# Expert weights in paired rows, a later combine, a spill from ScalarE's queue, and idle-time matmuls in a mixture-of-experts block

## The reference, cut to what matters

```python
h = rmsnorm(x, g_pre_ffn) * (1 + sc2) + sh2
logits = h @ w_router + b_router            # 256 x 32
top_v, top_i = lax.top_k(logits, 4)
gates = softmax(top_v)
# for each expert e, for the tokens that chose it:
gu = xblk @ w_gate_up[e] + b_gate_up[e]     # 1024 x 2048
x_glu = minimum(gu[:, :1024], 7.0)
x_lin = clip(gu[:, 1024:], -7.0, 7.0)
act = x_glu * sigmoid(1.702 * x_glu) * (x_lin + 1)
y = act @ w_down[e] + b_down[e]             # 1024 x 1024
out[token] += y * gate
x = x + gt2 * rmsnorm(out, g_post_ffn)
```

## Time and profile before

| | |
|---|---|
| median of 3 runs | 1250.05 us |
| profiled execution: its own time | 1251.14 us |
| its span, first to last instruction | 1249.1 us |
| PE (TensorE matmul) busy | 1037.8 us, 83% |
| PEld (weight load) busy | 496.9 us, 40% |
| DVE / ACT / POOL busy | 291.9 / 184.7 / 30.4 us |
| DMA moved | 464.63 MB, mean 372 GB/s |
| main DMA queue, share of 16 engines' span | 91.8% |
| chain that ended last | PE 52%, DMA 38%, DVE 4%, issue 3%, ACT 1% |
| mean granted TensorE clock | 0.935 |

### The profile page before, as it was taken

The page is one execution under the profiler, slowest core; times in us unless marked ns, Lnnn a source line. Parts: engine busy times, 40 slices in busy tenths (PEclk is TensorE's granted clock), DMA queues, the critical chain, the costliest instruction groups (busy, mean ns, idle before and its releaser), DMA issues.

```text
span 1249.1 us, 21341 instructions
## 1 busy us (share of the span) xinstructions
PE 1037.8 (83%) x8279; PEld 496.9 (40%) x8280; DVE 291.9 (23%) x786; ACT 184.7 (15%) x459; POOL 30.4 (2%) x52
## 2 busy tenths in 40 slices
PE   2799999977775999789979996999799979696965
PEld 0565878643332334324333433343334333232322
DVE  6646522142121111211121112112111211111112
ACT  0311354031011101011101110111011101100112
POOL 1000100130000000000000000000000000000000
PEclk9799999978888999989998999999899989898988
DMA  9979721977999969999999999999999999999996
GB/s 353 381 268 400 294 101 47 412 289 294 415 418 418 417 235 419 418 417 390 419 419 417 376 420 418 418 384 419 418 418 382 418 418 418 417 418 418 417 418 243
DMA packets 92208, 464.63 MB, mean 372 GB/s; under 512 B 5166, under 2 KB 6998, under 8 KB 59292
## 3 DMA queue, kind: packets, MB, share of 16 engines
q1 hardware_dynamic: 91740, 462.76, 91.8%
q0 software_dynamic: 448, 1.59, 0.3%
HBM read 462.22 MB, written 2.11 MB: 372 GB/s over the span
## 4 chain that ended last, share of the span: by engine, by line
PE 52%; DMA 38%; DVE 4%; issue 3%; ACT 1%; POOL 0%; DVEq 0%; SPq 0%; ACTq 0%; POOLq 0%
DMA arena<-in_w_down_dram 35%; PE pp L1402 15%; PE pp L1374 13%; PE pp L1182 4%; PE pp L1104 4%; DMA arena<-in_w_ada_dram 3%; PE po L1330 3%; PE pp L1195 2%; PE po L1247 2%; PE pp L1343 2%; PE pp L1363 2%; DVE arena L747 1%; PE pp L1382 1%; PE po L1062 1%; PE pp L1350 1%
## 5 line engine op out<-in xcount | busy, mean ns | idle before, releaser
L1374 PE MATMUL pp<-arena,work 128*32 128x256 f32 (+1 forms) x3840 | 360.1, 430 | 8.6 <-DMA arena<-in_w_gate_up_dram 8.6
L1402 PE MATMUL pp<-arena,work 128*32 128x256 f32 (+1 forms) x1920 | 217.7, 487 | 121.1 <-DMA arena<-in_w_down_dram 90.7
L1374 PEld LDWEIGHTS pp<-arena,work 128*32 128x32 f32 (+1 forms) x3840 | 155.8, 116 | 210.3 <-issue 140.7
L1402 PEld LDWEIGHTS pp<-arena,work 128*32 128x32 f32 (+1 forms) x1920 | 79.3, 128 | 220.3 <-DMA arena<-in_w_down_dram 111.1
L967 DVE TENSOR_SCALAR work<-pp 128x128 f32<-128x128 f32 (+1 forms) x74 | 25.3, 342 | 445.7 <-PE pp L1374 445.7
L669 ACT ACTIVATE work<-work 128x128 f32<-128x128 f32 (+1 forms) x74 | 25.9, 350 | 398.1 <-DVE work L967 398.1
L1343 PE MATMUL pp<-h_sb,work 128*32 128x256 f32 (+1 forms) x480 | 54.6, 462 | 34.1 <-issue 29.8
L1330 PE MATMUL po<-work 64*128 64x512 f32 x304 | 79.0, 640 | 1.6 <-ACT work L683 1.6
L961 DVE COPY work<-pp 128x256 f32<-128x256 f32 (+1 forms) x37 | 19.5, 526 | 234.7 <-PE pp L1343 234.7
L1182 PE MATMUL pp<-arena 128*128 128x256 f32 x256 | 57.4, 382 | 0.0
L747 DVE SCALAR_TENSOR_TENSOR arena<-arena,small 128x1024 f32<-128x1024 f32 x42 | 54.0, 1285 | 9.2 <-DMA arena<-in_w_ada_dram 7.7
(11 more groups left out here) (207 smaller groups left out, 643.7 us busy)
## 6 DMA issues: line engine op xcount, KB each, us to landing
arena<-in_w_gate_up_dram SPq DMA_DIRECT2D x128, 2048.0 KB, 25.6
arena<-in_w_down_dram SPq DMA_DIRECT2D x64, 2048.0 KB, 25.1
arena<-in_w_ada_dram SPq DMA_DIRECT2D x12, 2048.0 KB, 12.8
arena<-in_w_in_dram SPq DMA_DIRECT2D x5, 2048.0 KB, 15.7
arena<-in_w_gate_dram SPq DMA_DIRECT2D x4, 2048.0 KB, 14.2
arena<-in_w_out_dram SPq DMA_DIRECT2D x2, 2048.0 KB, 10.0
arena<-in_w_branch_a_dram SPq DMA_DIRECT2D x1, 2048.0 KB, 18.4
arena<-in_w_branch_b_dram SPq DMA_DIRECT2D x1, 2048.0 KB, 17.3
```

Of the source, the lines that this page charges most:

```text
L1374: mm = t_.matmul(pp[j * m:(j + 1) * m, UP[hh], 0:w].rearrange("p (s f) -> p s f", s=2), hgT[:, at:at + m], gu_w[slot][:, k, :, col:col + w ...
L1402: mm = t_.matmul(pp[j * m:(j + 1) * m, UP[0], 0:w], actT[:, at:at + m], wd[:, j * w:(j + 1) * w], start=(n == 0), stop=(n == KD - 1))
```

## The change

Six edits, made together:

- **Paired rows.** The contraction rows of an expert's matrices are dealt to partitions in pairs: partition p takes rows 256g + 2p and 256g + 2p + 1. A load of gate/up is then 128 runs of 16 KB in place of 256 of 8 KB, and a load of `w_down` 256 runs of 8 KB in place of 512 of 4 KB. The gathered tokens and the activations are turned in steps of two to match, and a narrow block's gate/up halves are the even and the odd columns: its moving operand is read with a step of two elements.
- **Order in a block.** `combine` and the turning of the scatter matrix move behind gate/up; the bias products move ahead of the turning of the tokens. `turn_half(1)` runs ahead of the down product. `actT` gets its own place. The bias is loaded twice, to two groups of rows (`hh`), so that the bias products of the halves stand in different rows.
- **Spill.** `x1` is written to DRAM from ScalarE's queue, after its squares, in place of SyncE's.
- **Tables.** `grids` moves from `bgu` into `gain2`; `gain2` (one row) is first written to DRAM by GpSimd and read back at the end (512 KB, behind `x1_back`). GpSimd makes the tables after its sums of the merged branches. DVE waits for them (`s_places`).
- **DVE order.** `first_part` stands ahead of the second `weigh` of its tile.
- **Products on idle TensorE.** `spin`: 16 products of zeros into `po` bank 0 in the routing chain, and 14 products into a free `pp` bank behind it.

```diff
 PAGE = 4096
+PAIR = 2 * P
...
-def bias_rows_of(slot):
-    return slice(32 + 64 * slot, 32 + 64 * slot + NBR)
+def bias_rows_of(slot, hh):
+    return slice(64 * slot + 32 * hh, 64 * slot + 32 * hh + NBR)
...
         bgu = sb("bgu", [96 + NBR, 2, BR])
-        grids = bgu[0:NEXP, :, :].rearrange("p s f -> p (s f)").rearrange("p (n e) -> p n e", e=NEXP)
+        grids = gain2[0:NEXP, 0:16 * NEXP].rearrange("p (n e) -> p n e", e=NEXP)
...
         hgT = work[:, 384:896]
-        actT = work[:, 384:896]
+        actT = work[:, 2176:2688]
...
-        gu_v = w_gate_up[0].rearrange("e (k p) n -> e p k n", p=P)
-        dn_v = w_down[0].rearrange("e (k p) n -> e p k n", p=P)
+        gu_v = w_gate_up[0].rearrange("e (g p r) n -> e p g (r n)", p=P, r=2)
+        dn_v = w_down[0].rearrange("e (g p r) n -> e p g (r n)", p=P, r=2)
...
             def load_bgu(slot, e):
-                sp.dma_start(bgu[bias_rows_of(slot), :, :], bgu_v[e]).then_inc(s_bgu[slot], 16)
+                for hh in range(2):
+                    sp.dma_start(bgu[bias_rows_of(slot, hh), :, :], bgu_v[e]).then_inc(s_bgu[slot], 16)
 
             def load_gu(slot, e, i):
-                sp.dma_start(gu_w[slot][:, 2 * i:2 * i + 2, :, :].rearrange("p k s f -> p k (s f)"),
-                             gu_v[e, :, 2 * i:2 * i + 2, :]).then_inc(s_gup[slot][i], 16)
+                sp.dma_start(gu_w[slot][:, 2 * i:2 * i + 2, :, :].rearrange("p k s f -> p (k s f)"),
+                             gu_v[e, :, i, :]).then_inc(s_gup[slot][i], 16)
...
             def load_dlo(slot, e):
-                sp.dma_start(dlo_w[slot], dn_v[e, :, 0:4, :]).then_inc(s_dlo[slot], 16)
+                sp.dma_start(dlo_w[slot].rearrange("p (g r) d -> p g (r d)", r=2),
+                             dn_v[e, :, 0:2, :]).then_inc(s_dlo[slot], 16)
 
             def load_dhi(e):
-                sp.dma_start(dhi_w, dn_v[e, :, 4:8, :]).then_inc(s_dhi, 16)
+                sp.dma_start(dhi_w.rearrange("p (g r) d -> p g (r d)", r=2), dn_v[e, :, 2:4, :]).then_inc(s_dhi, 16)
...
-            def spill_x1(t):
-                sp.wait_ge(s_x1, 2 * t + 2)
-                sp.dma_start(x1_dram[:, t, :], x_sb[:, t, :]).then_inc(s_spill, 16)
-
             sp.wait_ge(s_merged, KD)
             load_dlo(0, 0)
-            spill_x1(0)
             sp.wait_ge(s_wo0, 1)
             load_gu(0, 0, 3)
             page_free(sp, page_of("wo", 1))
             load_gu(1, 1, 0)
 
-            spill_x1(1)
             sp.wait_ge(s_spill, 16 * TT)
             sp.wait_ge(s_x1p, 2 * TT)
...
             sp.dma_start(x1_back, x1_dram[:, :, :]).then_inc(s_x1b, 16)
+            sp.dma_start(gain2[:], gain2_dram[0:1, :].to_broadcast([P, D])).then_inc(s_gback, 16)
...
                     a.activation(squares[half], x_sb[:, t, cols], ACT.Square,
                                  scale=float(D) ** -0.5,
                                  accum_out=ssq[:, 6 + 2 * t + half:7 + 2 * t + half]).then_inc(s_sqx, 1)
+                act.dma_start(x1_dram[:, t, :], x_sb[:, t, :]).then_inc(s_spill, 16)
                 act.wait_ge(s_sqx, 2 * t + 2)
                 act.wait_ge(s_part, 2 * t + 2)
                 a.activation(rms[:, 6 + t:7 + t], ssq[:, 7 + 2 * t:8 + 2 * t], ACT.Sqrt,
@@ -662,8 +669,6 @@
                     w = D * m // P
                     act.wait_ge(s_turn, it)
                     a.copy(hgT[:, 0:w], pp[:, TURN, 0:w]).then_inc(s_turned, 1)
-                    act.wait_ge(s_selT, it + 1)
-                    a.copy(selgT.rearrange("p t n -> p (t n)"), pp[:, TOKS, 0:TT * P]).then_inc(s_selTev, 1)
...
                         act.wait_ge(s_aT, halves[hh])
                         a.copy(actT[:, hh * w // 2:(hh + 1) * w // 2],
                                pp[:, (TOKS, TURN)[hh], 0:w // 2]).then_inc(s_aTev, 1)
+                    act.wait_ge(s_selT, it + 1)
+                    a.copy(selgT.rearrange("p t n -> p (t n)"), pp[:, TOKS, 0:TT * P]).then_inc(s_selTev, 1)
...
             def residual(t):
-                first_part(t, 0, 2, s_sqh)
                 link(rstd_of(t, 0))
...
             weigh(0, 0)
+            first_part(0, 0, 2, s_sqh)
             weigh(0, 1)
...
             choose(0)
+            first_part(1, 0, 2, s_sqh)
             weigh(1, 1)
...
             v.tensor_copy(wide_i, nblk_f[0:NEXP, 1, :]).then_inc(s_nblk, 1)
+            dve.wait_ge(s_places, 1)
             v.scalar_tensor_tensor(out=key, in0=pp[0:NEXP, 2, COUNT:COUNT + NEXP], scalar=float(NEXP), in1=key_add,
...
             dve.wait_ge(s_x1b, 16)
+            dve.wait_ge(s_gback, 16)
...
+            def spin(n):
+                for _ in range(n):
+                    t_.matmul(po[:, 0, :], zeros[:, 0:P], zeros, start=False, stop=False, skip_group_check=True)
+
+            spin(6)
             turn_x1(1)
+            spin(2)
             route(1)
+            spin(6)
             pe.wait_ge(s_chosen, TT)
             for col, table in ((RANK + NEXP, before), (COUNT, ones[:])):
                 mm = t_.matmul(pp[:, 2, col:col + NEXP], table, chosen[:, 1, :], start=False, stop=True,
                                skip_group_check=True)
             mm.then_inc(s_rank, 1)
 
+            spin(2)
             pe.wait_ge(s_gates, 1)
             for t in range(TT):
                 mm = t_.transpose(pp[0:NEXP, TURN, t * P:(t + 1) * P], gate_tab[:, t, :], ident[:])
             mm.then_inc(s_gT, 1)
+
+            index_halves = iota[:].bitcast(BF16)
+            for _ in range(14):
+                t_.matmul(pp[:, 0, :], ident[:].bitcast(BF16)[:, 0:P], index_halves, start=True, stop=True,
+                          skip_group_check=True)
             pe.wait_ge(s_bd, 32)
             pe.wait_ge(s_h2, 2 * TT)
             pe.wait_ge(s_nblk, 1)
@@ -1337,32 +1360,41 @@
                 tiles, w = P // m, D * m // P
...
+                def half_of(j, hh):
+                    return (2 * j + hh, slice(0, PAIR)) if w > PAIR else (j, slice(hh, PAIR, 2))
+
+                pe.wait_ge(s_bgu[slot], landed * 2)
                 pe.wait_ge(s_sel, it)
                 for t in range(TT):
                     for j in range(tiles):
+                        if (t, j) == (TT - 1, tiles - 1):
+                            pe.wait_ge(s_ysb, it + 1)
                         mm = t_.matmul(pp[j * m:(j + 1) * m, TOKS, 0:w], sel[:, t, 0:m],
                                        h_sb[:, t, j * w:(j + 1) * w], start=(t == 0), stop=(t == TT - 1))
                 mm.then_inc(s_hg, 1)
-                combine(it)
+
+
+                for j in range(tiles):
+                    for hh in range(2):
+                        rows = bias_rows_of(slot, hh)
+                        r, cols = half_of(j, hh)
+                        t_.matmul(pp[j * m:(j + 1) * m, UP[hh], 0:w].rearrange("p (s f) -> p s f", s=2),
+                                  pick[rows, r, 0:m], bgu[rows, :, cols], start=True, stop=False,
+                                  skip_group_check=True)
 
                 pe.wait_ge(s_hgs, it)
                 for i in range(q):
-                    mm = t_.transpose(pp[:, TURN, i * P:(i + 1) * P], hg[:, i * P:(i + 1) * P], ident[:])
+                    mm = t_.transpose(pp[:, TURN, i * P:(i + 1) * P],
+                                      hg[:, i // 2 * PAIR + i % 2:(i // 2 + 1) * PAIR:2], ident[:])
                 mm.then_inc(s_turn, 1)
-                pe.wait_ge(s_bgu[slot], landed)
-                pe.wait_ge(s_selg, it)
-                for t in range(TT):
-                    mm = t_.transpose(pp[:, TOKS, t * P:(t + 1) * P], selg[:, t, :, :].rearrange("p c j -> p (c j)"),
-                                      ident[:])
-                mm.then_inc(s_selT, 1)
-
-                rows = bias_rows_of(slot)
...
+                def turn_half(hh):
+                    pe.wait_ge(s_actv, halves[hh])
+                    for i in range(q // 2):
+                        mm = t_.transpose(pp[:, (TOKS, TURN)[hh], i * P:(i + 1) * P], sig[:, hh, i:w // 2:q // 2],
+                                          ident[:])
+                    mm.then_inc(s_aT, 1)
...
                         for j in range(tiles):
-                            col = j * w + hh * w // 2
+                            r, cols = half_of(j, hh)
                             mm = t_.matmul(pp[j * m:(j + 1) * m, UP[hh], 0:w].rearrange("p (s f) -> p s f", s=2),
-                                           hgT[:, at:at + m], gu_w[slot][:, k, :, col:col + w // 2], start=False,
-                                           stop=(k == KD - 1), skip_group_check=True)
+                                           hgT[:, at:at + m], gu_w[slot][:, k, :, r * PAIR:(r + 1) * PAIR][:, :, cols],
+                                           start=False, stop=(k == KD - 1), skip_group_check=True)
...
                 turn_half(0)
+                combine(it)
+                turn_half(1)
+                pe.wait_ge(s_aTev, halves[0])
+                pe.wait_ge(s_selg, it)
```

(10 more changed lines are left out.)

53 lines of the change are left out of this document (23 added, 30 removed).

## The result

The changed kernel takes 1230.62 us (median of 4 runs, 1229.40 to 1231.62) against 1249.67 us before (4 runs on the same chip, 1248.08 to 1252.39): ratio 0.9845, 95% interval 0.9825 to 0.9865. The forecast was 1221 us, range 1211 to 1238. The time lies in the range, but a third of the forecast gain of 29 us is missing.

A forecast was written before the change was run, and what follows sets the result against it. Saturated DMA (418 GB/s) bounds most expert loads, elsewhere a TensorE/DVE/ACT chain. Restart -4.3, experts -2.7 and -13.5, large stop -1, four stops -7, end -0.7: -29.2 from 1251.14, median 1.1 lower, so 1221 us; range 1211 to 1238.

The forecast's parts named there:

- Rows: Expert weight loads: 64 fewer rows per engine at about 10 ns each save 0.64 us an expert, net 0.54.
- Rival (1): Weight loads: the row cost isn't there for 16 KB runs or bytes are the limit; 1240 us, chance 0.15.
- The 0.1 us for the bias load: Expert loads: the second bias load costs between 0 and 0.17 us an expert, taken as 0.1.
- The four stops: Last four places where the DMA waits for TensorE: 1.7 us shorter each, 7 us in all, bounds 0 and 10.
- The first term: At each stop: `s_gu` 2.2 us earlier after the landing, less 0.3 for the second bias load, shrinks it 1.9 us.
- The second term: At each stop: the DMA, 0.35 us faster over its backlog of 8 MB, gives that back.
- First restart: DMA's return after the routing chain and first block: first `s_gu` 4.5 us earlier, loads restart 4.3 us earlier.
- The chain's 0.8 us: Routing chain: added products delay it, faster turns, `route` and `first_part` give time back; `s_nblk` comes 0.8 us earlier.
- rival (2): Routing chain: products cool and push, PE stays at low clock, first restart 2 us late; 1227 us, chance 0.12.
- clock 1.0 from 265 to 290: Sign for the routing chain and first block: TensorE at full clock from 265 to 290 us, first gate/up near 282.
- Before y5 and the end: Up to the sixth turn's upper `w_down` issue: restart -4.3, five experts -2.7, large stop -1 us; kernel's end: -0.7.
- Rival (3): Narrow blocks: the strided operand halves gate/up's rate, 7.11 to some 14.2 us; about 1300 us, chance 0.06.

The follow-up runs named there:

- e2: The kernel before with paired rows, and the turns and narrow halves they need, and nothing else: 1241.56 us, ratio 0.9923.
- e7: The changed kernel with `w_down` in rows of four, 16 KB runs instead of 8 KB; rows meet wrong activations, output differs: 1224.77 us, ratio 0.9803.
- e1: The changed kernel with its rows unpaired again (8 KB runs of gate/up, 4 KB of `w_down`), all other edits kept: 1245.72 us, ratio 0.9965.
- e3: The changed kernel with the bias loaded once, both halves' bias products reading the same rows: 1231.36 us, ratio 0.9842.
- e5: The changed kernel without any bias loads for experts after the first two, so the output differs: 1224.89 us, ratio 0.9795.
- e6: The changed kernel with narrow blocks reading gate/up and bias operands as whole 128-column halves, not every second column; output differs: 1229.19 us, ratio 0.9838.
- e8: The changed kernel with the next weights' first quarter issued after the second product of gate/up's second half, bias loads behind it: 1229.32 us, ratio 0.9835.
- e4: The changed kernel without its 30 added products on TensorE: 1230.34 us, ratio 0.9833.

## Why the prediction was right in kind and a third too large

- **Rows.** Right. Forecast 0.64 us an expert less 0.1 for the bias load, -13.5 us over the last 25 experts. The flat part lost 737.1 - 724.0 = 13.1. e2 and e7 put the price of a piece at about 9 ns; it was taken as 10. Rival (1) is not borne out. The 0.1 us for the bias load was a guess: e1 and e3 give 0.1, e5 less. The Trainium skill ("DMA: Bandwidth & Descriptors", section "Why small descriptors are slow (HBM only)") has about 3 bus cycles per packet, by the prediction's estimate 3.5 ns; the traces do not bear that out.
- **The four stops: the step that failed.** Forecast -7 us, measured -0.4. Each stop was to shrink by 1.9 us less 0.2 that the faster transfers take back (the prediction names 0.35 for it, but 0.9 of 2.6 left means 0.2). The first term had every piece of TensorE's order right (1.6 + 0.5 us) and the issue of the second bias load (0.4), but not the 0.38 us of the strided operand: 1.4 us by the profile. Without the stride, in e1, the first quarter is issued 17.0 us after the landing in three of the four stops, just the 1.9 us sooner that were forecast; but as flow e1 shows only 2.9 / 4 = 0.7, or about 1.1 if the 1.7 us of low clock in its fourth stop (where the issue comes after 18.65 us) are taken off. The second term was wrong: I set 0.35 us a stop, the backlog of 8 MB at a higher rate, and e2 shows 3.1 / 4 = 0.8. Of these 0.3 may be the strided operand's, which the rows bring along (e6: 10.3 to 9.1 over the four stops). In windows of 0.5 us the flow breaks 17.8 to 18.8 us after the landing in the four stops of before and 16.4 to 17.4 in those of after, 1.4 us sooner on average, though the bytes behind the landing are the same; that is all that the order had gained. How more than 0.35 us of it comes about is not shown. e8 shows why a larger gain on the first gate alone would have gone: 4.7 us behind it stands the second.
- **First restart.** Forecast -4.3 us, measured 295.92 to 293.17, -2.75. The block's order came out as worked out (2.6 us from gather to gate/up). The missing 1.5 us is gate/up at 8.95 instead of 7.11, by stride (0.4) and the clock's fall in its first microseconds (1.4). In the two profiles without either (e1, e6) the issue is at 291.6, the forecast value. The chain's 0.8 us came in part by luck: half of it stood at the chain's start, and e4 shows `route` fast without the products and the chain 1.1 us shorter. So rival (2) was right that they push, not that the clock stays low in the chain; the forecast sign "clock 1.0 from 265 to 290" failed at 282. Most of the line in the sum belongs to the block's order.
- **Before y5 and the end.** By y5 -5.6 us instead of -8.0, of which 1.5 is the restart and 0.9 the rest, within the scatter. The end gained 0.2 instead of 0.7: the last expert now waits 3.8 us for the landing of its gate/up weights, and the rest of its gate/up then takes 7.31 us at a clock of 0.50 where 4.52 were taken before, so it no longer waits for its `w_down`. In e1, where that rest takes 5.83 us, the end gained 0.8.
- **Rival (3)** names the right mechanism at the wrong stride: the factor is 1.05 at a stride of two, and 2 only at four.

Together: 2.4 + 0.4 + 6.6 + 0.5 = 9.9 us of missing gain, of forecast 29.2 against measured 19.3. The time lies in the range because that was drawn wide enough for rivals (1) and (2); it does not lie there by their mechanisms.
